# Dilated attention units issued one column tile earlier, with other PSUM banks and statistics in token order

## The chip, the cores and the metric

The kernel runs on one core of a Trainium2 chip. The metric is the device time of one execution in microseconds (us). Before the change it is 2284.05 us, the median of three runs (2281.86 to 2284.53).

## The reference, cut to what matters

A first block (a gated three-branch mixer over 512 tokens of width 1024) is followed by a second block of two layers. Only the attention part of each layer of the second block is touched:

```python
for l in range(2):
    h = rms_norm(x, norm_mix[l]); proj = h @ w_in[l]
    dq, dk, dv, sq, sk, sv, gate_logits = split(proj)      # dq, dk, dv: 3 groups x 4 heads x 64
    dq, dk = partial_rope(dq), partial_rope(dk)
    y_a = dilated_attention(dq, dk, dv) @ w_proj_a[l]       # merges 3 groups by softmax denominators
    y_b = stick_breaking_attention(sq, sk, sv) @ w_proj_b[l]
    gates = sigmoid(gate_logits + b_gate[l])
    mixed = gates[..., :1024] * y_a + gates[..., 1024:] * y_b
    x = x + mixed @ w_out[l]
    h = rms_norm(x, norm_ffn[l]); x = x + conv_ffn(h, ...)
```

Group 0 of the dilated attention looks at the last 129 tokens, group 1 at every 4th of the last 513, group 2 at every 16th. The kernel treats group 0 in token order, and groups 1 and 2 in "class" order: the tokens t = 4u + r with the same remainder r lie together.

## The kernel before, in words

Every big matrix product runs as three TensorE (PE) passes in fp32r, lines 1597 to 1599: weight-high by input-high, weight-high by input-low, weight-low by input-high. Weights come by DMA from the SyncE queue in chunks of two pieces (`chunk_load`); ScalarE (ACT) rounds a piece to its high half (`split_hi`, line 453), VectorE (DVE) subtracts to get its low half (`split_lo`, line 460), three pieces ahead of the tile that uses it. A piece is 24 matmuls of 512 columns (`col_tile`) or 48 of 256 columns (`token_tile`, for value tiles). Each engine's order of work is written out by hand; semaphores tie them. On PE, `give(bank, semaphore, value)` notes who reads a PSUM bank last, and the next `take(bank)` waits for that reader.

The order in a layer, on PE:

- 18 tiles (`DIL_KEYS`): six `dq`, six `dk`, six `dv` (two for each group 0, 1, 2). `dq` and `dk` tiles use banks 0 and 1 in turn; the value tiles of group 0 and of group 1 both use banks 0 and 1, those of group 2 use 4 and 5. Between them the stick-breaking attention of four heads runs: `sb_scores` (line 1807, banks 2 to 5), `sb_exponents` (1818, 1820), `sb_values` (1830, bank 6). ACT copies the value tiles out (line 882); those of groups 1 and 2 go to DRAM and come back in class order by a DMA from the POOL queue (line 621, awaited in `dil_values(0)`).
- `dil_scores(0)`, then eight units u (two head pairs j by four blocks b), two gate tiles each: gate tile 2u, `dil_transposes(u)` (line 1871), `dil_scores(u+1)` (1856, 1860), gate tile 2u+1, `dil_values(u)` (1889). Beside them DVE takes row maxima (`dil_max`, 1475 to 1478), ACT exponentiates (`dil_exp`, 905) and copies the transposed probabilities (`dil_pT`, 914). `dil_values` adds into bank 6 for group 0 (c = 0, 1) and bank 7 for groups 1 and 2 (c = 2, 3), both in blocks of 128 adjacent columns, so that bank 7 is in class order.
- In unit 7, `stat_rows` (1905) turns maxima and denominators into rows by 16 small matmuls. DVE's `shift_rows` and `share_rows` (1487 to 1503) and one ACT exponential make the two shares of each token, reordering between class and token order by strided reads and writes.
- Then the projections: `w_proj_b` half 0 (24 matmuls), `share_wide` (1917: four matmuls with 4 rows spread the shares over the partitions, banks 2 to 5), `w_proj_b` half 1, `w_proj_a` halves 0 and 1 (48 matmuls, line 1597 with `oaT`), and `row_tiles` of `w_out`. Between `share_wide` and `w_proj_a` lies a chain: ACT copies the wide shares from PSUM (941), DVE does a `split_lo`, then `dil_merge` (1509 to 1511) twice, ACT the high half (945), DVE the low half (`dil_lo`, 1515). Behind it DVE gates the `w_proj_b` results (1541), then those of `w_proj_a` (1547), adds both (1549), and takes the low half of the mix (1526).
- `w_proj_a` writes banks 2, 3, 4, 5, 0, 1, 6, 7 for m = 0 to 7. `row_tiles` first takes banks 0 to 3, so it waits until DVE has read m = 5 (line 1547).

## Time and profile before

| | us |
|---|---|
| runs, median (lowest to highest) | 2284.05 (2281.86 to 2284.53) |
| the profiled execution | 2284.14 |
| its span, first to last instruction | 2282.3 |
| PE busy | 2205.3 (97%) |
| DVE busy | 1258.1 (55%) |
| ACT busy | 779.2 (34%) |
| mean granted TensorE clock | 0.984 |

A busy PE is not PE at its peak: the ends of matmuls are modelled and overlap, so the pace of matmuls is read from the distance of their starts. The granted clock of 1.00 is 2.4 GHz, 0.50 is 1.2 GHz.

### The profile page before, as it was taken

The numbers are of one execution on the slowest core, as the hardware profiler recorded it, in microseconds if no ns is written. First come the engines' busy times: TensorE is split into PE (matmuls) and PEld (weight loads), VectorE is DVE, ScalarE is ACT, GpSimd is POOL, SyncE is SP. The second block draws the span as 40 slices with busy tenths as digits, with TensorE's granted clock in tenths as the row PEclk, the third lists the DMA queues.
The fourth block names the chain that finished last, engine by engine and source line by source line (L and its number), as shares of the span: only waits on it lengthen the run. The fifth ranks groups of instructions, "written<-read, shape, count | busy, mean of one in ns | idle before, by whom it ended". The sixth has DMA issues, their size and how long they took to land.

```text
span 2282.3 us, 25769 instructions
## 1 busy us (share of the span) xinstructions
PE 2205.3 (97%) x10730; PEld 1818.5 (80%) x10742; DVE 1258.1 (55%) x1662; ACT 779.2 (34%) x1112; POOL 35.4 (2%) x46
## 2 busy tenths in 40 slices
PE   3999999999999799999999999999999999999998
PEld 2788888888888697877788888889787768888887
DVE  7798797944655746323655554234632365555422
ACT  1223232223442344344343333134434424333211
POOL 1000000000000200000000000000000000000000
PEclk7999999999999899999999999999999989999999
DMA  8332322332222222222223223222222222332222
GB/s 303 116 103 90 108 97 79 111 110 94 88 97 97 74 93 74 90 79 73 74 75 111 92 94 107 86 83 93 74 94 78 69 74 74 101 103 93 95 99 74
DMA packets 188241, 217.91 MB, mean 95 GB/s; under 512 B 3808, under 2 KB 167262, under 8 KB 188126
## 3 DMA queue, kind: packets, MB, share of 16 engines
q1 hardware_dynamic: 184128, 210.52, 27.8%
q10 hardware_dynamic: 3262, 3.60, 0.5%
q8 instruction: 85, 1.39, 0.3%
q0 software_dynamic: 736, 2.15, 0.2%
q14 instruction: 30, 0.25, 0.0%
HBM read 212.06 MB, written 4.19 MB: 95 GB/s over the span
## 4 chain that ended last, share of the span: by engine, by line
PE 91%; DVE 6%; ACT 1%; issue 1%; POOL 0%; DMA 0%; SPq 0%; ACTq 0%; POOLq 0%; DVEq 0%
PE psum L1597 29%; PE psum L1599 28%; PE psum L1598 28%; DVE whl L460 1%; PE psum L1818 1%; DVE adsum L1038 1%; PE psum L1807 1%; PE psum L1830 1%; PE psum L1889 1%; PE psum L1860 1%; PE psum L1871 1%; DMA x<-in_x 0%; PE psum L1917 0%; DVE stat L1007 0%; ACT whl L453 0%
## 5 line engine op out<-in xcount | busy, mean ns | idle before, releaser
L1597 PE MATMUL psum<-hT,whl 128*128 128x512 f32 (+1 forms) x2112 | 804.4, 381 | 8.2 <-DVE hT L1060 5.4
L1598 PE MATMUL psum<-hT,whl 128*128 128x512 f32 (+1 forms) x2112 | 797.0, 377 | 0.0
L1599 PE MATMUL psum<-hT,whl 128*128 128x512 f32 (+1 forms) x2112 | 796.8, 377 | 0.0
L460 DVE TENSOR_TENSOR whl<-raw,whl 128x1024 fp32r<-128x1024 f32 (+1 forms) x368 | 449.3, 1223 | 594.4 <-ACT whl L453 594.4
L453 ACT ACTIVATE whl<-raw 128x1024 fp32r<-128x1024 f32 (+1 forms) x368 | 384.4, 1047 | 468.4 <-PE psum L1599 431.9
L1597 PEld LDWEIGHTS psum<-hT,whl 128*128 128x128 f32 x2112 | 399.0, 189 | 90.3 <-DVE hT L1060 8.9
L1599 PEld LDWEIGHTS psum<-hT,whl 128*128 128x128 f32 x2112 | 399.1, 189 | 73.4
L1598 PEld LDWEIGHTS psum<-hT,whl 128*128 128x128 f32 x2112 | 399.3, 189 | 71.3 <-issue 0.5
L1597 PE MATMUL psum<-whl,ff 128*128 128x512 f32 x352 | 139.2, 395 | 2.2 <-DVE fsil L1576 2.2
L1598 PE MATMUL psum<-whl,ff 128*128 128x512 f32 x352 | 138.9, 395 | 0.0
L1599 PE MATMUL psum<-whl,ff 128*128 128x512 f32 x352 | 138.9, 395 | 0.0
L1597 PE MATMUL psum<-whl,hT 128*128 128x256 f32 (+1 forms) x384 | 124.7, 325 | 10.3 <-DVE gates L1547 6.5
L1598 PE MATMUL psum<-whl,hT 128*128 128x256 f32 (+1 forms) x384 | 123.1, 321 | 0.0
L1599 PE MATMUL psum<-whl,hT 128*128 128x256 f32 (+1 forms) x384 | 123.0, 320 | 0.0
L1101 DVE SCALAR_TENSOR_TENSOR hc<-glu,vcol,hc 128x512 f32<-128x512 f32 x120 | 89.3, 744 | 0.0
L1597 PEld LDWEIGHTS psum<-whl,hT 128*128 128x128 f32 x384 | 73.6, 192 | 17.9 <-DVE gates L1547 7.3
L1567 DVE TENSOR_SCALAR facc<-apad,vcol 128x512 f32<-128x512 f32 x44 | 24.1, 547 | 110.9 <-ACT fsil L970 53.0
L1101 DVE SCALAR_TENSOR_TENSOR acc<-glu,vcol,acc 128x512 f32<-128x512 f32 x112 | 83.3, 744 | 0.1
L1597 PEld LDWEIGHTS psum<-whl,ff 128*128 128x128 f32 x352 | 66.3, 188 | 18.2 <-issue 3.0
L1598 PEld LDWEIGHTS psum<-whl,ff 128*128 128x128 f32 x352 | 66.3, 188 | 15.4
L1599 PEld LDWEIGHTS psum<-whl,ff 128*128 128x128 f32 x352 | 66.3, 188 | 15.4
L1599 PEld LDWEIGHTS psum<-whl,hT 128*128 128x128 f32 x384 | 73.7, 192 | 5.3
(270 smaller groups left out, 2159.4 us busy)
## 6 DMA issues: line engine op xcount, KB each, us to landing
raw<-in_w_in SPq DMA_DIRECT2D x88, 1024.0 KB, 5.1
raw<-in_w_up SPq DMA_DIRECT2D x44, 1024.0 KB, 5.1
raw<-in_w_down SPq DMA_DIRECT2D x20, 1024.0 KB, 5.1
ada<-in_w_ada SPq DMA_DIRECT2D x12, 1024.0 KB, 10.0
raw<-in_w_branch SPq DMA_DIRECT2D x12, 1024.0 KB, 5.1
raw<-in_w_out SPq DMA_DIRECT2D x12, 1024.0 KB, 5.0
x<-in_x SPq DMA_DIRECT2D x4, 512.0 KB, 6.7
v_by_token<-vnat ACTq DMA_DIRECT2D x4, 512.0 KB, 2.8
```

The source lines that it names most:

```text
L453: nc.scalar.activation(whl_view(w, 0), raw_view(w), ACT.Copy).then_inc(w_hi, 1)
L460: nc.vector.tensor_tensor(whl_view(w, 1), raw_view(w), whl_view(w, 0).bitcast(F), ALU.subtract).then_inc(w_lo, 1)
L1038: ins = V.scalar_tensor_tensor(o_, at_k(k), cact[:, k:k + 1], o_, ALU.mult, ALU.add)
L1101: last[dst is acc1] = step(V.scalar_tensor_tensor(A_(dst), g[:, k:k + SEQ], col("cf_w", 8 * k + tt), A_(dst), ALU.mult, ALU.add))
L1567: link(V.tensor_scalar(facc[:], apad[:, j, 2:2 + SEQ], cw(2), col("conv_b", FT * l + f), ALU.mult, ALU.add))
L1597: M(out_, stat_hi, mov_hi, start=start, stop=False, **kw)
L1598: M(out_, stat_hi, mov_lo, start=False, stop=False, **kw)
L1599: return M(out_, stat_lo, mov_hi, start=False, stop=stop, **kw)
L1807: M(bank(2 + kb)[:, 0:SEQ - kb * P], sbk[rows, h // 2, kb * P:(kb + 1) * P], sbq[rows, h // 2, kb * P:], start=True, stop=True, skip_group ...
L1818: M(bank(2 + kb)[:, (jb - kb) * P:SEQ - kb * P], (negtri_r if jb == kb else negones_r)[:], part[:, SBO[jb]:SBO[jb + 1]], start=False, stop ...
L1830: ins = M(bank(6)[po:po + HEAD, kb * P:], sbv[:, kb, h * HEAD:(h + 1) * HEAD], sba[:, SBO[kb]:SBO[kb + 1]], start=kb == 0, stop=kb == TB - ...
L1860: ins = M(bank(2 + e)[:, a:z], qd[heads, g, j, b * P:(b + 1) * P], kd[heads, g, j, k0:k0 + z - a], start=False, stop=g == 2, skip_group_ch ...
```

## The change

1. Value tiles come in the order of groups 1, 2, 0, and in banks 0 and 1, 6 and 7, 4 and 5. `dq` and `dk` tiles use banks 0 and 7. The stick-breaking output of head 3 goes to bank 0.
2. The dilated units are issued one column tile earlier: `dil_scores(0)` after value tile 16, `dil_transposes(0)` (into banks 6 and 7) and `dil_scores(1)` after value tile 17; then in unit u: gate tile 2u, `dil_values(u)`, gate tile 2u+1, `dil_transposes(u+1)`, `dil_scores(u+2)`. ACT's `dil_pT` and `dil_exp` and DVE's `dil_max` move with them.
3. `stat_rows` is cut in two: the maxima behind `dil_transposes(7)`, the denominators behind `dil_values(7)`, one gate tile before the projections. `share_rows` stands before the last `split_lo` of the gate tiles.
4. `dil_values` writes bank 7 in token order (a step of four elements in PSUM), and `stat_rows` does so for its second kind. The strided reads and writes on DVE go.
5. `dil_merge` reads the wide shares from PSUM: one product of 1024 elements and one sum per j in place of two products and a strided sum; ACT's copy (941) goes. Both merges stand before DVE's `split_lo`.
6. `w_proj_a` writes banks 2, 3, 0, 1, 4, 5, 6, 7.
7. In SBUF the constants and small tiles lie behind the scratch area in place of before it.

```diff
                 add("w_in_2", ("w_in_2", l, sec + g), [(name, l, g, j) for j in range(2)], 1024)
-        for g in range(3):
+        for g in (1, 2, 0):
...
-    PA_BANK = (2, 3, 4, 5, 0, 1, 6, 7)
+    PA_BANK = (2, 3, 0, 1, 4, 5, 6, 7)
+    SB_BANK = (6, 6, 6, 0)
+    PT_BANK = lambda u: 4 if u else 6
...
     def DIL_KEYS(l):
-        return [(name, l, g, j) for name in ("dq", "dk", "dv") for g in range(3) for j in range(2)]
+        return [(name, l, g, j) for name in ("dq", "dk", "dv") for g in ((1, 2, 0) if name == "dv" else (0, 1, 2)) for j in range(2)]
...
-        elif key[0] in ("dq", "dk", "gate"):
+        elif key[0] in ("dq", "dk"):
+            W_BANK[key] = 7 * key[-1]
+        elif key[0] == "gate":
...
         elif key[0] == "dv":
-            W_BANK[key] = 4 if key[2] == 2 else 0
+            W_BANK[key] = (4, 0, 6)[key[2]]
...
     whl = keep("whl", [P, 4, 2, 1024], R)
+    K = 1024
+    arena = at[0]
+    at[0] += ARENA
...
-    arena = (at[0] + 127) // 128 * 128
...
-    wide = over("wide", 12 * K, [P, 2, 2, SEQ])
+    wide = over("wide", 12 * K, [P, 2, SEQ])
...
+                    if n_ == 16:
+                        dil_exp(0)
+                    if n_ == 17:
+                        dil_pT(0)
+                        dil_exp(1)
 
                 for u in range(8):
                     split_hi(W[("gate", l, 2 * u)] + 3)
-                    dil_exp(u)
-                    if u == 4:
-                        dil_copy(0)
                     gate(2 * u)
-                    dil_pT(u)
+                    if u % 4 == 3:
+                        dil_copy(u // 4)
                     split_hi(W[("gate", l, 2 * u + 1)] + 3)
-                    if u == 7:
+                    gate(2 * u + 1)
+                    if u < 7:
+                        dil_pT(u + 1)
+                    if u < 6:
+                        dil_exp(u + 2)
+                    if u == 6:
                         act.wait_ge(row_x, l + 1)
                         A(mrow[0:4, 2:4, :], mrow[0:4, 2:4, :], ACT.Exp).then_inc(row_e, 1)
-                    gate(2 * u + 1)
-                dil_copy(1)
                 lead([("w_proj_b_2", l, 0)])
-                for j in range(2):
-                    act.wait_ge(wide_ps, 2 * l + j + 1)
-                    A(wide[:, j, :, :].rearrange("p a b -> p (a b)"), psum[:, (2 + 2 * j) * SEQ:(4 + 2 * j) * SEQ], ACT.Copy).then_inc(wide_in, 1)
                 lead([("w_proj_b_2", l, 1)])
                 for j in range(2):
                     act.wait_ge(oa_f, 2 * l + j + 1)
-                    A(oaT[:, j, 0, :], wide[:, j, 0, :], ACT.Copy).then_inc(oa_hi, 1)
+                    A(oaT[:, j, 0, :], wide[:, j, :], ACT.Copy).then_inc(oa_hi, 1)
...
-                    V.tensor_tensor(obT[po:po + HEAD, h // 2, 1, :], bank(6)[po:po + HEAD, :],
+                    V.tensor_tensor(obT[po:po + HEAD, h // 2, 1, :], bank(SB_BANK[h])[po:po + HEAD, :],
...
+                row = lambda i_: mrow[0:4, i_, :]
+
+                def shift_rows():
+
+                    dve.wait_ge(row_ps, 2 * l + 1)
+                    link(V.tensor_copy(row(0), bank(2)[0:4, :]))
+                    link(V.tensor_tensor(row(1), row(0), bank(3)[0:4, :], ALU.min))
+                    step(V.tensor_tensor(row(2), row(1), row(0), ALU.subtract))
+                    V.tensor_tensor(row(3), row(1), bank(3)[0:4, :], ALU.subtract).then_inc(row_x, 1)
+
+                def share_rows():
+
+                    dve.wait_ge(row_ps, 2 * l + 2)
+                    dve.wait_ge(row_e, l + 1)
+                    V.tensor_tensor(mrow[0:4, 0:2, :], mrow[0:4, 2:4, :], psum[0:4, 4 * SEQ:6 * SEQ].rearrange("p (a b) -> p a b", a=2),
+                                    ALU.mult).then_inc(den_used, 1)
+                    dve.wait_ge(den_used, l + 1)
+                    link(V.tensor_tensor(row(0), row(0), row(1), ALU.add))
+                    link(V.reciprocal(row(0), row(0)))
+                    step(V.tensor_tensor(row(4), row(2), row(0), ALU.mult))
+                    V.tensor_tensor(row(5), row(3), row(0), ALU.mult).then_inc(share, 1)
+
+                def dil_merge(j):
+
+                    dve.wait_ge(wide_ps, 2 * l + j + 1)
+                    dve.wait_ge(o_copied, 2 * l + j + 1)
+                    V.tensor_tensor(osb[j][:], osb[j][:], psum[:, (2 + 2 * j) * SEQ:(4 + 2 * j) * SEQ].rearrange("p (a b) -> p a b", a=2),
+                                    ALU.mult).then_inc(wide_used, 1)
+                    dve.wait_ge(wide_used, 2 * l + j + 1)
+                    V.tensor_tensor(wide[:, j, :], osb[j][:, 0, :], osb[j][:, 1, :], ALU.add).then_inc(oa_f, 1)
+
+                def dil_lo(j):
+                    dve.wait_ge(oa_hi, 2 * l + j + 1)
+                    V.tensor_tensor(oaT[:, j, 1, :], wide[:, j, :], oaT[:, j, 0, :].bitcast(F), ALU.subtract).then_inc(oa_lo, 1)
...
-
-                    dve.wait_ge(row_ps, 2 * l + 1)
-                    link(V.tensor_copy(by_token(row(0)), by_class(bank(3)[0:4, :])))
-                    link(V.tensor_tensor(row(1), bank(2)[0:4, :], row(0), ALU.min))
-                    step(V.tensor_tensor(row(2), row(1), bank(2)[0:4, :], ALU.subtract))
-                    V.tensor_tensor(row(3), row(1), row(0), ALU.subtract).then_inc(row_x, 1)
-
...
-                def share_rows():
-
-                    dve.wait_ge(row_ps, 2 * l + 2)
-                    dve.wait_ge(row_e, l + 1)
-                    step(V.tensor_tensor(row(1), row(2), bank(4)[0:4, :], ALU.mult))
-                    V.tensor_tensor(by_token(row(0)), by_token(row(3)), by_class(bank(5)[0:4, :]), ALU.mult).then_inc(den_used, 1)
-                    dve.wait_ge(dve_chain, chain[0])
-                    dve.wait_ge(den_used, l + 1)
-                    link(V.tensor_tensor(row(1), row(1), row(0), ALU.add))
-                    link(V.reciprocal(row(1), row(1)))
-                    step(V.tensor_tensor(row(4), row(2), row(1), ALU.mult))
-                    V.tensor_tensor(by_class(row(5)), by_token(row(3)), by_token(row(1)), ALU.mult).then_inc(share, 1)
-
-                def dil_merge(j):
-
-                    dve.wait_ge(wide_in, 2 * l + j + 1)
-                    dve.wait_ge(o_copied, 2 * l + j + 1)
-                    step(V.tensor_tensor(osb[j][:, 0, :], osb[j][:, 0, :], wide[:, j, 0, :], ALU.mult))
-                    link(V.tensor_tensor(osb[j][:, 1, :], osb[j][:, 1, :], wide[:, j, 1, :], ALU.mult))
-                    V.tensor_tensor(by_token(wide[:, j, 0, :]), by_token(osb[j][:, 0, :]), by_class(osb[j][:, 1, :]), ALU.add).then_inc(oa_f, 1)
...
+                    if n_ >= 16:
+                        dil_max(n_ - 16)
 
                 for u in range(8):
                     split_lo(W[("gate", l, 2 * u)] + 3)
-                    dil_max(u)
                     if u == 7:
+                        share_rows()
+                    split_lo(W[("gate", l, 2 * u + 1)] + 3)
+                    if u < 6:
+                        dil_max(u + 2)
+                    if u == 6:
                         shift_rows()
-                    split_lo(W[("gate", l, 2 * u + 1)] + 3)
-                share_rows()
+
                 def mixed_lo(m):
                     dve.wait_ge(mix_hi, 8 * l + m + 1)
                     V.tensor_tensor(hT[:, 1, m, :], gates[:, m, :], hT[:, 0, m, :].bitcast(F), ALU.subtract).then_inc(mix_lo, 1)
 
 
                 for j in range(2):
-                    split_lo(W[("w_proj_b_2", l, j)] + 3)
                     if j:
                         for jj in range(2):
                             dil_merge(jj)
+                    split_lo(W[("w_proj_b_2", l, j)] + 3)
+                    if j:
                         for jj in range(2):
                             dil_lo(jj)
...
                     pe.wait_ge(p_ready, 8 * l + u + 1)
-                    take(4, 5)
+                    tb = PT_BANK(u)
+                    take(tb, tb + 1)
...
-                            ins = nc.tensor.transpose(bank(4 + e)[:, c * P:(c + 1) * P], prob[:, e, c * P:(c + 1) * P], ident)
...
-                            ins = M(bank(6 + c // 2)[e * HEAD:(e + 1) * HEAD, b * P:(b + 1) * P], v, probT[:, e, c * P:(c + 1) * P],
+                            o_ = bank(6 + c // 2)[e * HEAD:(e + 1) * HEAD, :]
+                            o_ = o_[:, b * P:(b + 1) * P] if c < 2 else by_token(o_)[:, b, :]
+                            ins = M(o_, v, probT[:, e, c * P:(c + 1) * P],
                                     start=c in (first_, 2), stop=c in (1, 3), skip_group_check=True)
...
-                def stat_rows():
-
-                    pe.wait_ge(p_ready, 8 * l + 8)
-                    take(2, 3)
-                    for n_, columns in enumerate((nmax, den)):
-                        if n_:
-                            take(4, 5)
-                        for kind in range(2):
-                            for b in range(TB):
-                                ins = M(bank(2 + 2 * n_ + kind)[0:4, b * P:(b + 1) * P], columns[:, kind, b, :], ident, start=True, stop=True,
-                                        skip_group_check=True)
-                        ins.then_inc(row_ps, 1)
-                    give(2, row_x, l + 1)
-                    give(4, den_used, l + 1)
+                by_token = lambda ap: ap.rearrange("p (u r) -> p r u", r=TB)
+
+                def stat_rows(n_, columns):
+
+                    if n_ == 0:
+                        pe.wait_ge(p_ready, 8 * l + 8)
+                    take(2 + 2 * n_, 3 + 2 * n_)
+                    for b in range(TB):
+                        M(bank(2 + 2 * n_)[0:4, b * P:(b + 1) * P], columns[:, 0, b, :], ident, start=True, stop=True, skip_group_check=True)
+                    for r in range(TB):
+                        ins = M(by_token(bank(3 + 2 * n_)[0:4, :])[:, r, :], columns[:, 1, r, :], ident, start=True, stop=True, skip_group_check=True)
+                    ins.then_inc(row_ps, 1)
+                    give(2 + 2 * n_, *((den_used, l + 1) if n_ else (row_x, l + 1)))
...
@@ -1917,18 +1921,38 @@
                             ins = M(bank(2 + 2 * j + kind), sel[0:4, j, :], mrow[0:4, 4 + kind, :], start=True, stop=True)
                         ins.then_inc(wide_ps, 1)
                         for kind in range(2):
-                            give(2 + 2 * j + kind, wide_in, 2 * l + j + 1)
-
-                dil_scores(0)
+                            give(2 + 2 * j + kind, wide_used, 2 * l + j + 1)
+
+                for n_, key in enumerate(DIL_KEYS(l)):
+                    if key[0] == "dv":
+                        token_tile(key)
+                    else:
+                        col_tile(key, h_at(0), h_at(1))
+                    h, ph = n_ // 4, n_ % 4
+                    if ph == 0 and h >= 1:
+                        sb_values(h - 1)
+                    if ph == 0 and h < 4:
+                        sb_scores(h)
+                    if ph == 2 and h < 4:
+                        sb_exponents(h)
+                    if n_ == 16:
+                        dil_scores(0)
+                    if n_ == 17:
+                        dil_transposes(0)
+                        dil_scores(1)
+
                 for u in range(8):
                     col_tile(("gate", l, 2 * u), h_at(0), h_at(1))
-                    dil_transposes(u)
+                    dil_values(u)
+                    if u == 7:
+                        stat_rows(1, den)
+                    col_tile(("gate", l, 2 * u + 1), h_at(0), h_at(1))
                     if u < 7:
-                        dil_scores(u + 1)
-                    else:
-                        stat_rows()
-                    col_tile(("gate", l, 2 * u + 1), h_at(0), h_at(1))
-                    dil_values(u)
+                        dil_transposes(u + 1)
+                    if u < 6:
+                        dil_scores(u + 2)
+                    if u == 6:
+                        stat_rows(0, nmax)
```

## Rows read from the trace of the kernel before

**Rows 1.** Page, part 1 and part 4: busy time by engine, chain that ended last.
```profile
PE 2205.3 (97%) x10730; PEld 1818.5 (80%) x10742; DVE 1258.1 (55%) x1662; ACT 779.2 (34%) x1112; POOL 35.4 (2%) x46
PE 91%; DVE 6%; ACT 1%; issue 1%; POOL 0%; DMA 0%; SPq 0%; ACTq 0%; POOLq 0%; DVEq 0%
```
**Rows 2.** Waits of PE, whole span: waiting line, releaser: us in total, times, longest.
```profile
PE psum L1597 <- DVE gates L1547: 6.5, 2, 4.1
...
PE psum L1597 <- DVE oaT L1515: 3.1, 2, 2.2
PE psum L1597 <- ACT vd L882: 2.3, 2, 1.2
...
PE psum L1597 <- ACT qraw L873: 1.5, 2, 0.7
```
**Rows 3.** Timeline of PE, projections of layer 0: start, us, instructions [idle before, releaser].
```profile
1089.95 3.83 PE L1917 MATMUL psum<-mrow,cst 4*128 4x512 f32 x8
1093.71 0.80 PE L1597 MATMUL psum<-obT,whl 128*128 128x512 f32 x1
...
1103.09 0.51 PE L1597 MATMUL psum<-oaT,whl 128*128 128x512 f32 x1 [2.15 <-DVE oaT L1515]
...
1118.56 0.47 PE L1597 MATMUL psum<-whl,hT 128*128 128x512 f32 x1 [2.48 <-DVE gates L1547]
1118.86 0.39 PE L1598 MATMUL psum<-whl,hT 128*128 128x512 f32 x1
1119.09 0.40 PE L1599 MATMUL psum<-whl,hT 128*128 128x512 f32 x1
```
**Rows 4.** Timeline of PE, the same places of layer 1.
```profile
1831.01 4.20 PE L1917 MATMUL psum<-mrow,cst 4*128 4x512 f32 x8
1835.14 0.79 PE L1597 MATMUL psum<-obT,whl 128*128 128x512 f32 x1
...
1844.55 0.50 PE L1597 MATMUL psum<-oaT,whl 128*128 128x512 f32 x1 [0.94 <-DVE oaT L1515]
...
1860.02 0.76 PE L1597 MATMUL psum<-whl,hT 128*128 128x512 f32 x1 [4.06 <-DVE gates L1547]
```
**Rows 5.** Windows: stretch, us, busy PE PEld DVE ACT POOL, granted clock, DMA, GB/s.
```profile
1093.80:1103.00 9.20, 7.14 (x24) 5.40 (x24) 7.02 (x10) 3.92 (x5) 0.00 (x0) 0.84 0.00 0
1103.00:1118.50 15.50, 12.99 (x48) 10.10 (x48) 14.25 (x23) 4.38 (x7) 0.00 (x0) 0.89 0.20 68
...
1835.10:1844.50 9.40, 8.51 (x25) 6.37 (x24) 7.09 (x10) 3.96 (x5) 0.00 (x0) 0.69 0.00 1
...
1860.00:1875.00 15.00, 14.98 (x56) 12.18 (x57) 8.54 (x12) 4.96 (x6) 0.00 (x0) 0.84 0.20 71
```
**Rows 6.** Groups by form, 963 to 1132 us: busy us, mean ns, idle before, releaser.
```profile
L460 DVE TENSOR_TENSOR whl<-raw,whl 128x1024 fp32r<-128x1024 f32 x23 | 28.0, 1223 | 91.1 <-ACT whl L453 91.1
...
L1526 DVE TENSOR_TENSOR hT<-gates,hT 128x512 fp32r<-128x512 f32 x8 | 5.5, 685 | 0.1
...
L1511 DVE TENSOR_TENSOR wide<-osb 128x512 f32<-128x512 f32 x2 | 2.1, 1067 | 0.1
...
L1487 DVE COPY mrow<-psum 4x512 f32<-4x512 f32 x1 | 0.7, 678 | 5.1 <-PE psum L1905 5.1
```
**Rows 7.** Chain that ended last, in order of time: start, us, what.
```profile
993.26 1.02 PE psum L1889 x16
...
1073.94 3.59 PE psum L1905 x32
```
**Rows 8.** Timeline of DVE and ACT, layer 0, from the last value tiles to unit 0.
```profile
935.90 1.49 DVE L1451 TENSOR_TENSOR splo<-sbs,sphi 128x1280 fp32r<-128x1280 f32 x1 [1.70 <-ACT sphi L853]
...
967.54 0.42 DVE L1475 TENSOR_REDUCE stat<-psum 128x2 f32<-128x256 f32 x1
...
970.30 0.21 ACT L905 ACTIVATION_READ_ACCUMULATOR prob<-psum,stat 128x1 f32 x1
```
**Rows 9.** Page, part 6: DMA issues: count, KB each, us from issue to landing.
```profile
vc<-v_by_token POOLq DMA_DIRECT2D x4, 512.0 KB, 6.1
```

105 lines of the change are left out of this document (45 added, 60 removed).

## The prediction

> **What bounds the kernel now.** Read busy time and the chain first: PE is busy 97% of the span and makes 91% of the chain that ended last [rows 1]. So only what PE waits for, what PE itself does and its clock can move the time. The waits of PE come next: in the stages touched there are four, each once per layer [rows 2]. The timelines place them [rows 3, 4]: behind `share_wide`, w_proj_a waits for DVE's last low half of `oaT` (2.15 us in layer 0, 0.94 in layer 1), and `row_tiles` of w_out for the DVE line 1547 (2.48 and 4.06). The other two are the bank waits in front of value tiles: for ACT's copy of the tile before (line 882) and for `qraw` (line 873). Last the windows with the granted clock [rows 5]: behind `share_wide` and behind two of the waits PE runs partly at 0.50, the level of 1.2 GHz. The matmuls of 512 columns start 0.23 us apart at full clock (1118.86 to 1119.09 in rows 3).
>
> The sum is made against the profiled execution, 2284.14 us (span 2282.3 and 1.8 around it). The median of the runs is 2284.05, so the two need no correction.
>
> **Banks of the value tiles.** Group 1 starts in banks 0 and 1, whose last reader is now two tiles back (dk half 0; half 1 went to bank 7), so the 1.5 us for line 873 go. Group 2 goes to 6 and 7, group 0 to 4 and 5, last read by head 3's exponentials a tile earlier: the 2.3 us for line 882 go. Together **3.8 us** [rows 2]. What is late next: ACT now has to drain and issue the DMA of group 1 (two instructions) in front of head 3's `sphi`. DVE's `splo` comes behind it and ends at 937.4 [rows 8], while PE still has a value tile of 48 half-width matmuls, about 24 x 0.23 = 5.5 us, to run. A delay of well under 1 us there is hidden; if it were not, it would be paid once per layer. POOL's DMA back takes 6.1 us [rows 9] and starts two tiles earlier against its reader, so its cover grows.
>
> **Units one tile ahead.** No instruction is added or dropped on PE. In a unit the chain is scores, maxima, exponentials, transposes. From the first maximum to the end of the last exponential it took 970.5 - 967.5 = 3.0 us for unit 0 [rows 8], and about 4 us for a full unit. Before it had one gate tile (24 x 0.23 = 5.5 us) with a `split_lo` in front on DVE; now it has two tiles and `dil_values`, over 12 us. For unit 0 only value tile 17 is between, and DVE's `sb_out(3)` (0.7 us) stands in front: 0.7 + 3.0 is under 5.5. These chains cost PE next to nothing before, so I count 0 to 0.4 us, taken as **0**. The moved waits have work behind them: `dil_exp(u+1)` on ACT is in front of `split_hi` of a piece that PE wants three tiles later, over 16 us; the SyncE queue reloads `raw` behind that split, up to some 6 us later than before, and a chunk has that slack twice. `share_rows` on DVE (about 7 us, a 3.3 us reciprocal in it) stands in front of the split of the first w_proj_a piece, wanted after w_proj_b and `share_wide`, over 12 us later. The shares are ready a gate tile earlier; `share_wide` did not wait before, so this alone gives nothing.
>
> **The merge chain.** Let P be the start of `share_wide` (1089.95). Before, w_proj_a started at P + 13.1. Now DVE starts at P + 2.0 with a product of 1024 elements from PSUM. Its price is bounded by `split_lo` of that size, 1.22 us [rows 6], and twice that; I take the first, since a DVE copy of 512 elements from PSUM takes 0.68 like a sum of 512 from SBUF [rows 6]. Product 1.2 and sum 0.7 (without the stride: 0.69 for 1.07, rows 6), twice: P + 5.9. `split_lo` 1.2, two low halves 0.6 each: P + 8.4. PE ends `share_wide` at P + 3.76 [rows 3] and needs 24 x 0.23 = 5.5 more for w_proj_b: P + 9.3, at half clock later. So DVE is done 0.9 us before PE asks: the 3.1 us go.
>
> **Banks of w_proj_a.** `row_tiles` takes banks 0 to 3, read now by m = 0 to 3 and not m = 5. DVE: four gatings of w_proj_b until P + 11, a split to P + 12.2, then three instructions of about 0.63 us per m. It has read m = 3 by P + 18, and the second low half of the mix, which the first block wants, is there by P + 17.3. PE arrives at P + 9.3 + 11.1 = P + 20.4. The later low halves come every 1.9 us; PE uses two in 5.5 us. So the 6.5 us go too. Sum of both waits: **9.6 us** [rows 2].
>
> **The clock behind the waits.** Lost time in a window is (1 - granted) x length. Layer 0, w_proj_a behind its wait: 0.11 x 15.5 = 1.7 us; layer 1, w_out behind the 4.06 us: 0.16 x 15.0 = 2.4 us [rows 5]. The clock fell after PE had stood still, so without the waits I take back all: **4.1 us**; the bounds are 0 and 4.1. Behind `share_wide` the loss is 0.16 x 9.2 = 1.5 and 0.31 x 9.4 = 2.9 us [rows 5]. Its 4-row matmuls stay, so I leave these 4.4 us; they could go (-4.4), or double (+4.4).
>
> **Token order written by PE.** Half of the value instructions and half of the statistics now write PSUM with a step of four elements. No row shows such a write. Priced at a factor f: a unit's 16 value instructions take 1.02 us and the 32 of the statistics 3.59 [rows 7], so (0.51 x 8 + 1.80) x 2 layers = 11.8 us x (f - 1). Below 1 is excluded: the instructions and columns are the same. From above, DVE's strided write to SBUF is 1067 ns for 685, f = 1.56 [rows 6]: 6.6 us; and the strided read from PSUM cost nothing (678, line 1487). I take f = 1: the statistics' instruction takes 3.59 / 32 = 112 ns for 128 columns, twice the time per column of the 512-column ones (0.23 us), so a write at half pace would still keep up. That is the weakest step.
>
> The Trainium skill speaks against it (Advanced Engine Details and Errata, section PSUM Cachelines): PSUM lines hold two fp32 values, and a non-contiguous pattern "significantly slows down matmuls". It gives no factor. No row here shows it right or wrong.
>
> **Constants behind scratch.** Addresses alone; the tiles of one operation in different buffers take the same time in all rows read. 0.
>
> **Sum.** 3.8 + 9.6 + 4.1 = 17.5; 2284.14 - 17.5 = 2266.6, and **2266.5 us** against the median.
>
> **Rivals.**
> - Strided writes cost moderately, f from 1.5 to 2. For: DVE's row; the token-order write is read out of no row. Against: the slow pace per column of these instructions. 2266.5 + 5.9 to 11.8 = 2272 to 2278.
> - Slower than before: strided writes cost much. It decides from 11.8 x (f - 1) = 17.5, f = 2.5. At f = 4 (every fourth element, four times the lines) it is +35.4: 2302 us. Against: nothing in the rows comes near it. This is where the skill's rule would lead if "significantly" is a factor over 2.5.
> - The wait only moves: w_proj_a or w_out still waits for DVE, because the merge chain has 0.9 us to spare and a late share or a PSUM product at double price (+2.4 us) eats it. Half of 9.6 stays, and with it the 4.1 of clock: 2266.5 + 8.9 = 2275.
> - The clock goes otherwise behind `share_wide`: 4.4 us back, 2262; or 4.4 more, 2271.
>
> **How the numbers follow.** Forecast 0.52; moderate cost 0.18; wait moves 0.12; clock otherwise 0.11 (0.07 down, 0.04 up); slower 0.07. The forecast's own range is 2263 to 2270. Eight in ten: 2262 to 2278, which leaves out the slow rival and the ends of the others. A measurement of this kernel can't tell under 0.2%, 4.6 us, from no change. Faster, under 2279.5: all but the slow rival and a mix of costs, 0.88. Same 0.05, slower 0.07.
>
> **What would show it.** Waits of PE on lines 873, 882, 1515 and 1547 gone in both layers; w_proj_a starting about 9.5 to 12 us after `share_wide` starts, and w_out 11.1 us later; clock 1.00 in both windows. In the chain of waits, 16 instructions of `dil_values` still at 1.02 us and the statistics at 1.8 us a half: any more is f. Wrong would be: a new PE wait on `prob` or `probT` between gate tiles, on `whl` (a split or a chunk late), or on `vc`.

## The result, and the profile after

The changed kernel takes 2254.14 us (median of 4 runs, 2253.38 to 2254.63) against 2283.06 (2281.86 to 2284.53) of the kernel before beside it: a ratio of 0.9873, 95% interval 0.9856 to 0.989. It is faster, and by more than forecast: 2254.1 lies below the range of 2262 to 2278. The profiled execution took 2254.25 (span 2252.4), 29.9 us less than the one of before.

Page of the kernel after, parts 1 and 4 (they answer to [rows 1]):

```profile
PE 2188.2 (97%) x10742; PEld 1816.0 (81%) x10742; DVE 1257.7 (56%) x1656; ACT 775.2 (34%) x1108; POOL 35.4 (2%) x46
PE 92%; DVE 5%; issue 1%; ACT 1%; DMA 1%; POOL 0%; SPq 0%; POOLq 0%; DVEq 0%; ACTq 0%
```

PE's busy time fell by 17.1 us. Waits that go don't lower busy time; matmuls that no longer run at half clock do, and so does a faster pace. The runs told of below part the two: the change without its layout has 2199.1 us of PE busy, the layout alone 2195.3.

Waits of PE, whole span, after (answers to [rows 2]; columns as there). The lines shown were there before and lie outside the change; the four of [rows 2] are gone:

```profile
PE psum L1725 <- DVE adsum L1048: 13.7, 4, 4.8
...
PE psum L1611 <- DVE hT L1070: 6.1, 4, 4.4
PE psum L1611 <- DVE fsil L1590: 2.2, 2, 1.1
PE psum L1611 <- POOL hT L612: 1.5, 1, 1.5
PE psum L1611 <- DVE whl L467: 0.9, 3, 0.3
PE psum L1729 <- DVE stat L1061: 0.5, 1, 0.5
```

Timeline of PE and DVE in the projections of layer 0, after (answers to [rows 3]; the three passes are now lines 1611 to 1613):

```profile
1082.48 4.88 PE L1921 MATMUL psum<-mrow,cst 4*128 4x512 f32 x8
1087.29 0.80 PE L1611 MATMUL psum<-obT,whl 128*128 128x512 f32 x1
1087.88 0.63 PE L1612 MATMUL psum<-obT,whl 128*128 128x512 f32 x1
...
1094.94 0.39 PE L1611 MATMUL psum<-oaT,whl 128*128 128x512 f32 x1
...
1105.82 0.39 PE L1611 MATMUL psum<-whl,hT 128*128 128x512 f32 x1
```
```profile
1084.49 1.22 DVE L1504 TENSOR_TENSOR osb<-osb,psum 128x1024 f32<-128x1024 f32 x1 [1.22 <-PE psum L1921]
...
1087.39 1.22 DVE L1504 TENSOR_TENSOR osb<-osb,psum 128x1024 f32<-128x1024 f32 x1 [0.95 <-PE psum L1921]
...
1090.39 1.29 DVE L1511 TENSOR_TENSOR oaT<-wide,oaT 128x512 fp32r<-128x512 f32 x2
```

The product from PSUM takes the 1.22 us that was chosen for it. The last low half of `oaT` ends at 1091.7, 3.3 us before PE starts w_proj_a at 1094.94, and w_out follows 10.88 us later with no wait (11.1 was forecast). Counted from the start of `share_wide`, DVE is ready after 9.2 us (8.4 forecast) and PE asks after 12.5 (9.5 to 12 forecast): `share_wide` took 1.1 us longer than before, and the passes behind it ran at half clock.

Windows of the projections, after (columns as in [rows 5], which they answer to). Behind `share_wide` the clock is still at half; in w_proj_a and w_out it is now 1.00 in both layers:

```profile
1087.00:1092.00 5.00, 5.00 (x13) 3.71 (x13) 4.57 (x6) 0.73 (x2) 0.00 (x0) 0.53 0.00 0
...
1817.00:1822.00 5.00, 5.00 (x13) 3.92 (x12) 4.43 (x7) 0.63 (x1) 0.00 (x0) 0.50 0.00 0
```
```profile
1094.90:1105.80 10.90, 10.90 (x49) 9.02 (x49) 9.02 (x14) 4.54 (x6) 0.00 (x0) 1.00 0.28 96
1105.80:1120.80 15.00, 15.00 (x68) 12.41 (x67) 12.94 (x17) 5.50 (x7) 0.00 (x0) 1.00 0.19 57
1824.60:1835.50 10.90, 10.90 (x49) 9.03 (x49) 8.99 (x14) 4.54 (x6) 0.00 (x0) 1.00 0.26 96
1835.50:1850.50 15.00, 15.00 (x68) 12.39 (x67) 12.96 (x17) 5.50 (x7) 0.00 (x0) 1.00 0.17 60
```

The writes in token order can be read in one kernel, side by side. Timeline of PE, the statistics of the maxima, after (answers to [rows 7]): line 1909 writes adjacent columns, line 1911 every fourth.

```profile
1061.01 1.04 PE L1909 MATMUL psum<-cst,stat 128*4 128x128 f32 x8
1061.88 1.04 PE L1911 MATMUL psum<-cst,stat 128*4 128x128 f32 x8
```

Both take 1.04 us, and the 16 value instructions stand in the chain of waits at their old 1.02:

```profile
980.53 1.02 PE psum L1894 x16
```

What is left is in stages that no edit touches. Tile `ff` (the input of the second half of the feed-forward), the kernel before and then the kernel after: durations in ns, lowest, median and highest, of the passes that read it:

```profile
L1597 PE MATMUL psum<-whl,ff x352: 390/393/475, 1408.6 to 2274.4; 128*128 128x512 f32 x176
```
```profile
L1611 PE MATMUL psum<-whl,ff x352: 387/389/476, 1395.7 to 2244.5; 128*128 128x512 f32 x176
```

The durations are modelled, so the number to read is how many start in equal time. Window of these matmuls alone, before and then after: stretch, us, PE busy (count), clock, DMA, GB/s:

```profile
1420.00:1470.00 50.00, 50.00 (x217) 1.00 0.28 95
```
```profile
1420.00:1470.00 50.00, 50.00 (x223) 1.00 0.29 95
```

That is 6 more passes in the same 50 us at the same granted clock: their starts are 232 ns apart before and 227 after (medians over 1055 distances, each from a pass on `ff` to the matmul behind it). The 1055 distances add to 245.5 us before and 239.6 after, 2.4% less.

Where the 30 us went, by the starts of matmuls on PE (us, layers 0 and 1 together; worked out from the profiled executions, one of each kernel. "Start" is the first pass with a weight tile, 53 us into the span. The other columns are the runs told of below):

```
stretch                                        before   after  layout  no layout  banks   banks   merge
                                                               only    (e2)       w_proj  value   only
                                                               (e1)               (e7)    (e8)    (e9)
start to the stick-breaking of layer 0         781.8   776.9   776.9   781.7     781.9   781.9   782.1
stick-breaking scores to share_wide            510.5   504.4   510.3   504.8     510.5   505.3   510.4
share_wide to w_out                             57.6    46.6    58.0    45.7      51.2    59.2    50.9
w_out to the first pass on ff                  582.4   579.8   584.1   579.9     580.0   583.1   585.5
first pass on ff to the next layer / the end   297.2   291.4   291.4   297.2     297.2   298.2   297.2
sum                                           2229.5  2199.1  2220.7  2209.3    2220.7  2227.7  2226.1
```

### The profile page after: what moved, and what is told of

It reads as the page before. It is cut to its first block, busy times and chain, and to the rows that moved or that the text cites. A ratio compares the mean times of both kernels' runs of the same rounds, so it can differ in the third digit from the quotient of the medians.

```text
span 2252.4 us, 25769 instructions
## 1 busy us (share of the span) xinstructions
PE 2188.2 (97%) x10742; PEld 1816.0 (81%) x10742; DVE 1257.7 (56%) x1656; ACT 775.2 (34%) x1108; POOL 35.4 (2%) x46
## 4 chain that ended last, share of the span: by engine, by line
PE 92%; DVE 5%; issue 1%; ACT 1%; DMA 1%; POOL 0%; SPq 0%; POOLq 0%; DVEq 0%; ACTq 0%
PE psum L1611 29%; PE psum L1612 29%; PE psum L1613 29%; PE psum L1832 1%; DVE adsum L1048 1%; PE psum L1821 1%; PE psum L1845 1%; DVE whl L467 1%; PE psum L1862 1%; PE psum L1894 1%; PE psum L1874 1%; PE psum L1921 0%; DMA x<-in_x 0%; DVE stat L1017 0%; POOL stat L617 0%
## 5 line engine op out<-in xcount | busy, mean ns | idle before, releaser
L1611 PE MATMUL psum<-whl,ff 128*128 128x512 f32 x352 | 137.3, 390 | 2.2 <-DVE fsil L1590 2.2
L1612 PE MATMUL psum<-whl,ff 128*128 128x512 f32 x352 | 137.0, 389 | 0.0
L1613 PE MATMUL psum<-whl,ff 128*128 128x512 f32 x352 | 137.0, 389 | 0.0
L1611 PEld LDWEIGHTS psum<-whl,ff 128*128 128x128 f32 x352 | 66.1, 188 | 16.7 <-issue 3.0
L1611 PEld LDWEIGHTS psum<-whl,hT 128*128 128x128 f32 x384 | 73.2, 191 | 5.4
L1613 PEld LDWEIGHTS psum<-whl,ff 128*128 128x128 f32 x352 | 66.1, 188 | 13.8
L1613 PEld LDWEIGHTS psum<-whl,hT 128*128 128x128 f32 x384 | 73.1, 190 | 5.0
L1612 PEld LDWEIGHTS psum<-whl,hT 128*128 128x128 f32 x384 | 73.2, 191 | 5.0
```

The source lines that it names most:

```text
L1611: M(out_, stat_hi, mov_hi, start=start, stop=False, **kw)
L1612: M(out_, stat_hi, mov_lo, start=False, stop=False, **kw)
L1613: return M(out_, stat_lo, mov_hi, start=False, stop=stop, **kw)
```

## The experiments

The kernel before ran beside each group of runs and gave medians of 2285.91 (the runs up to the one with all 128 up), 2282.19 (64 up and the parts alone) and 2286.18 (256 up, the probe and the split). Its single executions lie between 2281.6 and 2287.9, so a difference of a few us between two kernels is read from the ratio and its interval, not from two medians.

**The layout alone.** Theory: point 7 of the change made the passes faster. Rival: something else in the change did.

```diff
+    ARENA = 80 * 1024 + 16704 + 2112
...
     whl = keep("whl", [P, 4, 2, 1024], R)
+    arena = at[0]
+    at[0] += ARENA
...
-    arena = (at[0] + 127) // 128 * 128
```

> The kernel before with point 7 of the change alone: the scratch area directly behind the weight buffers, constants and small tiles behind it. Theory A (the miss of the prediction is this point): in the trace before, 512-column passes whose one operand lies in the scratch area start 232 to 233 ns apart, those with both operands outside it 227 ns; after, all are at 227. This kernel then gains about 12 us: 2283 to about 2271, and its passes on yahl and ff start 227 ns apart, while the four PE waits of the prediction stay. Theory B (the layout is nothing, and the extra came from units one tile ahead or from the merge): no change, 2283.

Measured: 2276.01 us, ratio 0.996 (0.9946 to 0.9974). The window of `ff`:

```profile
1420.00:1470.00 50.00, 50.00 (x223) 1.00 0.28 95
```

The pace is the one of after, and two of the table's stretches (the first, and the one from `ff` on) fall by the same 4.9 and 5.8 us as in the change. Its waits stay. The stretch from `w_out` to `ff` is 1.7 us longer; that is the clock, and the kernels with other addresses, told of below, show that such a difference comes and goes with no change in the order of work.

**The change without the layout.**

```diff
-    arena = at[0]
-    at[0] += ARENA
...
+    arena = (at[0] + 127) // 128 * 128
```

> The kernel after with point 7 undone: constants in front, scratch area where it was. Theory A: the rest of the change is worth what the prediction summed, 17.5 us, so about 2266, and the passes on yahl and ff are back at 232 ns. Theory B: stays at 2254.

Measured: 2263.27 us, ratio 0.9904 (0.9889 to 0.9918). `ff` is back at the old pace:

```profile
1420.00:1470.00 50.00, 50.00 (x216) 1.00 0.27 95
```

By the sums of the table, points 1 to 6 give 20.2 us and point 7 gives 10.2; the forecast had 17.5 and 0. By the medians and ratios of the runs, points 1 to 6 give 22 (18.7 to 25.4), and the layout 9 to 12 (2263.27 against 2254.14; and the layout alone and the two kernels with 128 bytes, told of next, against the kernel before).

**What about the addresses?** By the kernel's allocation, `hT` begins at byte 32896 of a partition and `whl` at 82048, both 128 above a multiple of 256. The scratch area (`ff`, the mixer's tiles, `oaT`, `obT`) begins at 128000 before, a multiple of 256, and at 114816 after, 128 above one. Theory A1 (A1a in some of the expectations): what counts is the distance of a matmul's two operands modulo 256 bytes (128 is slow, 0 is fast). A1b: what counts is the absolute place of the one in scratch. Four kernels before, with the scratch area moved by 128 and 256 and 64 bytes, and with everything moved by 128 and scratch on a multiple of 256.

```diff
-    arena = (at[0] + 127) // 128 * 128
+    arena = (at[0] + 127) // 128 * 128 + 128
```

> The kernel before with the scratch area 128 bytes higher and nothing else. Before, the scratch area starts at a multiple of 256 bytes and hT and the weight buffers 128 bytes behind one. Theory A1 (the pace hangs on the addresses modulo 256): all passes at 227 ns, about 2271. Theory A2 (it hangs on where the scratch area lies in the memory as a whole, above or beside the constants): no change, 2283.

```diff
-    base = (nc.sbuf_base + 63) // 64 * 64
+    base = (nc.sbuf_base + 63) // 64 * 64 + 128
...
-    arena = (at[0] + 127) // 128 * 128
+    arena = (at[0] + 255) // 256 * 256
```

> The kernel before with x, hT, raw and the weight buffers 128 bytes higher, so that they start at multiples of 256 bytes, and the scratch area at a multiple of 256 too. Theory A1a (both operands of a pass must have the same address modulo 256, whichever it is): all passes at 227 ns, about 2271. Theory A1b (the absolute address counts: an operand at a multiple of 256 is slow): now every pass on hT is slow as well, 5568 + 384 of 512 columns at 5 ns each, some 30 us more than before, about 2313.

```diff
-    arena = (at[0] + 127) // 128 * 128
+    arena = (at[0] + 127) // 128 * 128 + 256
```

> The kernel before with the scratch area 256 bytes higher alone: distance from hT and the weight buffers 128 bytes modulo 256 as before, but every address of it moved twice as far as in the 128-byte run. Theory A1 (period of 256 bytes): passes on ff and yahl stay at 232 ns, time about 2283. Rival (any move off the old place helps, the old place being bad for another reason): 227 ns, about 2272.

```diff
-    arena = (at[0] + 127) // 128 * 128
+    arena = (at[0] + 127) // 128 * 128 + 64
```

> The kernel before with the scratch area 64 bytes higher alone; its distance from hT and the weight buffers is then 192 bytes modulo 256. Theory A1a in its plain form (only a distance of 0 modulo 256 is fast): passes with one operand in the scratch area stay at about 232 ns, time about 2283. Rival (any distance but 128 is fast, or distance 0 modulo 64 is all that counts): 227 ns and about 11 us less.

Measured, the window of `ff` in each. Scratch 128 up (2274.6 us, ratio 0.9954, 0.9938 to 0.997), then all 128 up (2273.79, 0.9951, 0.9935 to 0.9967):

```profile
1420.00:1470.00 50.00, 50.00 (x222) 1.00 0.30 98
```
```profile
1420.00:1470.00 50.00, 50.00 (x222) 1.00 0.28 96
```

Scratch 256 up (2282.35 us, one execution), then 64 up (2280.84, one execution):

```profile
1420.00:1470.00 50.00, 50.00 (x217) 1.00 0.28 95
```
```profile
1420.00:1470.00 50.00, 50.00 (x220) 1.00 0.29 95
```

128 bytes alone bring the whole gain (10.7 us from the first matmul to the last), and 256 bytes bring none. With everything 128 up, scratch is again on a multiple of 256, where it was slow before, and the pace is fast: A1b falls, A1 stands. The 64 bytes gave `ff` a pace between the two (229 ns median; the 1055 distances add to 241.8 us), which neither form of the theory had in it, while the tiles of the mixer stayed at 233: it is not a matter of two cases.

One tile of the scratch area tests A1 once more, inside single kernels. `poolhl` lies 64 bytes above a multiple of 256 where the rest of scratch lies on one. Its 512-column passes start 233.4 ns apart in the kernel before (64 bytes below `whl` modulo 256) and 230.8 in the kernel after (64 above), so it never was at the best pace. With scratch 64 up it comes to distance 0 as the only scratch tile, and there it is at 226.7 ns, beside 233.3 for `yahl` in the same kernel (means of 40 and 176 distances).

These kernels also show how far the clock moves by itself. The order of work between `share_wide` and `ff` is that of the kernel before in the layout alone and in the four address kernels, and the two stretches together took 640.0 us (before), 642.1 (layout alone), 639.4 (128 up), 642.0 (all 128 up), 637.1 (256 up) and 639.9 (64 up): 5.0 us from the lowest to the highest, of which the address effect makes about 1. Windows of PE in layer 1, the kernel before and then 256 up (stretch, us, PE busy (count), clock, DMA, GB/s):

```profile
1820.00:1880.00 60.00, 55.00 (x217) 0.89 0.20 70
```
```profile
1820.00:1880.00 60.00, 55.54 (x230) 0.94 0.21 71
```

The kernel after does the same in its two profiled executions: 626.4 us, and 624.8 when it was run again. So of a single execution's stretches between `share_wide` and `ff`, a difference of 2 us or so is not the edit's until more runs show it.

**The parts that take waits away, each alone.** First the banks of w_proj_a (point 6):

```diff
-    PA_BANK = (2, 3, 4, 5, 0, 1, 6, 7)
+    PA_BANK = (2, 3, 0, 1, 4, 5, 6, 7)
```

> The kernel before with point 6 alone (w_proj_a writes banks 2, 3, 0, 1, 4, 5, 6, 7). By the prediction: the waits of 2.48 and 4.06 us in front of w_out go and the half clock behind the second, 2.4 us, with them: 8.9 us less. Rival: w_out then waits for the low halves of the mix in place of the banks (the wait only moves), and at most 2 to 4 us are gained.

Measured: 2275.9 us (2274.35 to 2278.04), ratio 0.997 (0.9957 to 0.9982), which is 4 to 10 us. The sum of the table falls by 8.8 us, as expected. The wait for the gatings is gone, and `w_out` to `ff` is 2.4 us shorter with no half clock behind `w_out`; but with scratch 256 up, where that wait stayed (4.9 us in two), there was none behind `w_out` either, so these 2.4 us are not shown to be the edit's. The wait for `oaT` stays, and the clock is at half for a while behind it in layer 0 (0.89), not in layer 1 (1.00). Waits of PE, then the windows behind that wait in either layer:

```profile
PE psum L1597 <- DVE oaT L1515: 3.5, 2, 2.1
```
```profile
1103.00:1118.00 15.00, 14.53 (x56) 11.70 (x57) 13.78 (x21) 4.45 (x7) 0.00 (x0) 0.89 0.20 70
...
1845.00:1860.00 15.00, 15.00 (x67) 12.21 (x66) 13.75 (x21) 4.75 (x7) 0.00 (x0) 1.00 0.20 71
```

Then the banks of the value tiles (point 1):

```diff
+    SB_BANK = (6, 6, 6, 0)
...
-        elif key[0] in ("dq", "dk", "gate"):
+        elif key[0] in ("dq", "dk"):
+            W_BANK[key] = 7 * key[-1]
+        elif key[0] == "gate":
...
-            W_BANK[key] = 4 if key[2] == 2 else 0
+            W_BANK[key] = (4, 0, 6)[key[2]]
```

> The kernel before with point 1 alone (order and banks of the value tiles, banks of dq and dk, bank of head 3). By the prediction 3.8 us less; measured from start to start instead of by idle time, the two gaps are 1.44 - 0.12 and 1.12 - 0.23 us, so 2.2 us a layer, 4.4 us less. Rival: the two DMAs now issued by ACT earlier delay head 3 and eat it: 0 to 2 us.

Measured: 2281.39 us (2280.01 to 2283.29), ratio 0.9993 (0.9983 to 1.0002): by the runs no difference that can be told. Its own stretch falls by 5.2 us in the table, more than expected, but the profiled execution is 3.3 us longer elsewhere: the projections by 1.6, `w_out` to `ff` by 0.7, the last stretch by 1.0. In the projections it is the clock, which here falls inside `share_wide` already, as it did in the layout alone, where no bank was changed. That the value banks cause it is not shown, and the last stretch is not explained. Windows of layer 0, this kernel and then the one before:

```profile
1089.00:1094.00 5.00, 5.00 (x11) 2.23 (x10) 0.00 (x0) 2.47 (x3) 0.00 (x0) 0.68 0.30 115
1094.00:1099.00 5.00, 5.00 (x16) 3.98 (x15) 4.41 (x6) 1.15 (x2) 0.00 (x0) 0.64 0.00 0
```
```profile
1089.00:1094.00 5.00, 5.00 (x14) 2.19 (x13) 1.40 (x3) 1.21 (x2) 0.00 (x0) 0.94 0.60 209
1094.00:1099.00 5.00, 5.00 (x17) 3.95 (x17) 3.15 (x4) 1.78 (x2) 0.00 (x0) 0.72 0.00 0
```

Last the merge chain (point 5):

```diff
-                for j in range(2):
-                    act.wait_ge(wide_ps, 2 * l + j + 1)
-                    A(wide[:, j, :, :].rearrange("p a b -> p (a b)"), psum[:, (2 + 2 * j) * SEQ:(4 + 2 * j) * SEQ], ACT.Copy).then_inc(wide_in, 1)
...
-                    step(V.tensor_tensor(osb[j][:, 0, :], osb[j][:, 0, :], wide[:, j, 0, :], ALU.mult))
-                    link(V.tensor_tensor(osb[j][:, 1, :], osb[j][:, 1, :], wide[:, j, 1, :], ALU.mult))
+                    V.tensor_tensor(osb[j][:], osb[j][:], psum[:, (2 + 2 * j) * SEQ:(4 + 2 * j) * SEQ].rearrange("p (a b) -> p a b", a=2),
+                                    ALU.mult).then_inc(wide_in, 1)
```

> The kernel before with point 5 alone, in class order: dil_merge multiplies 1024 elements straight from PSUM, ACT's copy goes, both merges stand before split_lo; the strided sum stays. By the prediction's chain the low halves are ready 4.6 us earlier, w_proj_a no longer waits, and w_out still waits for the bank of m = 5, but that comes 4.6 us earlier too: 7 to 10 us less. Points 5 and 6 share one DVE chain, so their separate gains sum to more than both together (13.7 by the prediction). Rival: the product from PSUM costs double, 2.4 us later: 3 to 5 us less.

Measured: 2281.74 us (2278.71 to 2284.18), ratio 0.9989 (0.998 to 0.9998), far less than expected. The wait for `oaT` goes, and from `share_wide` to w_out 6.7 us go with it. But w_out is reached earlier against the same gatings and waits 3.24 us in layer 0, where it was 2.48 (in layer 1 3.2, where it was 4.06; 6.5 in all as before). Behind it the clock is at half in both layers, before in layer 1 alone. Timeline of PE at that place and the window behind it:

```profile
1116.32 0.77 PE L1596 MATMUL psum<-whl,hT 128*128 128x512 f32 x1 [3.24 <-DVE gates L1546]
1116.88 0.63 PE L1597 MATMUL psum<-whl,hT 128*128 128x512 f32 x1
```
```profile
1117.00:1122.00 5.00, 5.00 (x13) 3.85 (x12) 4.84 (x8) 2.41 (x4) 0.00 (x0) 0.50 0.00 0
```

13 matmuls are counted in these 5 us, where 23 or so would be at 227 ns. `w_out` to `ff` is 3.2 us longer than before. Over the two stretches from `share_wide` to `ff`, points 5 and 6 alone so give 3.6 and 8.8 us, 12.4 in all; with both in (e2) they give 14.4, 625.6 against 640.0. That difference of 2.0 us is within what the clock does by itself, so these sums don't show that the parts need one another.

The times of the runs say it better. The three parts alone have ratios of 0.9993, 0.9970 and 0.9989, some 11 us in all; points 1 to 6 together have 0.9904, some 22, and points 2 to 4 show no gain of that size in any stretch. So the parts are worth more together than one by one. The reading that fits is that the half clock comes back only when the last wait near it goes: PE was at half clock between `share_wide` and `ff` for 20.5 us in the kernel before, 13.7 in e7, 23.9 in e8, 20.5 in e9 and 10.2 in e2, and half of such a time is lost. It rests on one execution of each, and 256 up had 13.7 with both waits in place; so it is argued, not shown.

**A probe of step and offset.** In front of w_proj_b, additional matmuls whose results nobody reads: 64 in bf16 with 256 adjacent columns in PSUM, 64 with every second column; then nine blocks of 32 in fp32r with 448 columns, with the stationary and the moving operand begun at various columns of `hT` (4 bytes each).

```diff
+                for o_ in (bank(6)[:, 0:256], bank(6).rearrange("p (n t) -> p t n", t=2)[:, 0, :]):
+                    for _ in range(64):
+                        M(o_, identb[:], maskb[:, 0:256], start=True, stop=True, skip_group_check=True)
+                for so, mo in ((0, 0), (0, 8), (0, 16), (0, 24), (0, 32), (0, 48), (0, 64), (32, 0), (32, 32)):
+                    for _ in range(32):
+                        M(bank(6)[:, 0:448], hT[:, 0, 0, so:so + P], hT[:, 1, 2, mo:mo + 448], start=True, stop=True, skip_group_check=True)
```

> The kernel after with matmuls added in front of w_proj_b in each layer, their results not used. First 64 bf16 matmuls of 256 columns to adjacent PSUM columns and 64 to every second column. If a step of two costs (each element on its own 8-byte line), the second 64 start about twice as far apart, some 215 ns for 107; if not, both take the same. Then nine blocks of 32 fp32r matmuls of 448 columns, stationary and moving operand both in hT, with the moving one 0, 32, 64, 96, 128, 192 and 256 bytes further, then the stationary one 128 bytes further, then both. Theory A1: with distance 0 and 256 and with both moved the starts are 448/512 of 227 ns apart, 198 to 199; with 128 bytes, whichever operand moves, some 2% more, 203; 64 and 192 bytes between or above. Rival (the absolute address of one operand counts): the block with both moved is slow too, and one of the two 128-byte blocks is fast.

Measured (2409.81 us, one execution; what counts are the windows, one for each block, in order: bf16 adjacent, bf16 every second, then the nine offsets):

```profile
1077.95:1084.95 7.00, 7.00 (x65) 6.27 (x65) 3.43 (x4) 1.63 (x2) 0.00 (x0) 1.00 0.34 106
1084.95:1098.58 13.63, 13.63 (x66) 8.78 (x65) 0.00 (x0) 0.00 (x0) 0.00 (x0) 1.00 0.07 26
1098.58:1105.25 6.67, 6.67 (x34) 6.21 (x33) 0.00 (x0) 0.00 (x0) 0.00 (x0) 1.00 0.00 0
1105.25:1111.87 6.62, 6.62 (x33) 6.02 (x32) 0.00 (x0) 0.00 (x0) 0.00 (x0) 1.00 0.00 0
1111.87:1118.26 6.39, 6.39 (x33) 5.99 (x32) 0.00 (x0) 0.00 (x0) 0.00 (x0) 1.00 0.00 0
...
1124.83:1131.36 6.53, 6.53 (x33) 6.01 (x32) 0.00 (x0) 0.00 (x0) 0.00 (x0) 1.00 0.00 0
...
1137.82:1144.43 6.61, 6.61 (x33) 6.01 (x32) 0.00 (x0) 0.00 (x0) 0.00 (x0) 1.00 0.00 0
```

The step costs a factor of 1.97 here: starts are 109.3 ns apart with adjacent columns and 215.2 with a step of two, the same in both layers. So a stepped write does cost, where a matmul writes a column in 0.43 ns. With the step it takes 0.84 ns for each, and the fp32 statistics, at 109 ns for 128 columns, take 0.85 with or without one. This fits the reason that the prediction gave for f = 1: a write at half pace keeps up with these matmuls. The two sides differ in more than pace, though (bf16 and a step of two, fp32 and a step of four). By the Trainium skill (Advanced Engine Details and Errata, section PSUM Cachelines) a non-contiguous pattern slows matmuls significantly: the bf16 rows agree, the fp32 rows of this kernel don't. fp32r matmuls with a step were not tried.

The offsets matter in the probe too, with paces from 200.0 to 206.7 ns, but not as A1 has it (the windows shown are those of 0, 8, 16, 32 and 64 columns): no offset took 202.7, 16 columns (64 bytes) 200.0, 32 columns (128 bytes) 203.7, and 64 columns (256 bytes) 206.7, as slow as any. With both operands begun 32 columns further it was 206.5, where the same distance without the shift took 202.7. Here every matmul loads the same stationary tile, where the passes of the kernel change it. So A1 holds for the passes of this kernel, by five layouts and `poolhl`, and is no general law; why the addresses matter stays open.

**share_wide in two halves.** To break up the stretch of 4-row matmuls: two of the four behind half of w_proj_b half 0, two behind its end.

```diff
-                def share_wide():
+                def share_wide(j):
...
+                        if mm == 2 and between is not None:
+                            between()
...
-                projection("w_proj_b_2", 0, PB_BANK, obT, pb_ps, pb_f)
-                share_wide()
+                projection("w_proj_b_2", 0, PB_BANK, obT, pb_ps, pb_f, lambda: share_wide(0))
+                share_wide(1)
```

> The kernel after with share_wide cut in two: the four matmuls of j = 0 (with 4 rows each) between the second and third quarter of the first half of w_proj_b, those of j = 1 behind that half. After, PE runs at 0.50 of its clock behind share_wide in both layers and loses 2.4 and 3.4 us there. If the unbroken 4 us of nearly empty matmuls bring the clock down, the two halves of 2 us do not, and 4 to 6.5 us are gained: about 2248 to 2250 against the kernel after on the same chip. If their sum counts, nothing is gained.

Measured: 2251.96 us (2249.1 to 2256.1), ratio 0.9856 (0.9841 to 0.9871). Beside it, the kernel after once more:

> The kernel after unchanged, for comparison with the others on the same chip: 0.987 of the kernel before.

2254.08 us (2253.35 to 2254.71), ratio 0.9865 (0.9848 to 0.9881): the result repeats to 0.1 us. The two can't be told apart. The half clock does not go; it comes behind either half, and the windows of layer 0's projections show both:

```profile
1084.00:1089.00 5.00, 5.00 (x13) 2.80 (x12) 2.45 (x3) 1.06 (x1) 0.00 (x0) 0.75 0.36 139
1089.00:1094.00 5.00, 5.00 (x16) 3.91 (x16) 4.93 (x8) 1.26 (x2) 0.00 (x0) 0.66 0.00 0
```

In its profiled execution, the slowest of its four, the way from the first pass of w_proj_b to w_out is 29.25 us in layer 0 and 29.27 in layer 1; in the kernel after it is 28.87 and 28.79, and in that kernel run again 28.80 and 27.24. The others of the split ran at a mean clock of 0.988 to 0.99 against its 0.986, so the split may let the clock come back earlier at times; that is argued from the clocks, not shown.

## Why the prediction was wrong, point by point

**The step that failed** is the one on constants behind scratch: "Addresses alone; the tiles of one operation in different buffers take the same time in all rows read. 0." The runs showed 10.2 us in its place (e2 against the kernel after; 9 to 12 by the runs), since the passes on the scratch area run faster with both operands at the same place modulo 256 bytes. The trace of before did hold the difference: passes on `ff` and on the mixer's tiles start 232 ns apart and those on `hT` 227, with the same shape, clock and type. The prediction read 0.23 us off two rows on `hT` [rows 3], and to two decimals both paces are the same. 5 ns over the 2064 passes that read a scratch tile are 10 us. The sum over all 1055 distances on `ff`, divided by their count, would have shown it. Which way a new layout would turn this was not to be known from one trace, but that it could move by about 10 us either way was, and no rival had it.

**Banks of the value tiles**: 3.8 forecast, 5.2 measured in their own stretch (e8). The waits went as described. The size was off since an idle time in a row of waits is counted from the modelled end of the matmul before, not from the start that it could have had: for line 882 the row has 1.16 us, while the start comes 1.44 behind the last one where 0.12 is the pace, so 1.32. Likewise the 0.73 us for line 873 are 0.89 by starts. About 0.3 us per layer more lies between the first dilated scores and values and was not traced.

**Units one tile ahead**: 0 forecast. With these points, the stepped writes among them, the stretch is 0.5 us shorter than with the banks alone (504.8 in e2, 505.3 in e8), which one execution of each can't tell from nothing. Right.

**The merge chain, the banks of w_proj_a and the clock behind the waits**: 9.6 + 4.1 = 13.7 forecast, 14.4 measured from `share_wide` to `ff` (e2). The waits went as described. The agreement to 0.7 us is in part luck, since kernels with one order of work differ by up to 5 us over these stretches. The margin in front of w_proj_a was 3.3 us and not 0.9, because PE came late, and not because DVE was early: DVE was 0.8 us later than forecast, its second product having waited 0.95 us for `share_wide`. At full clock PE would have asked 9.3 us after the start of `share_wide` by the forecast's sum, and DVE was ready at 9.2. The half clock behind `share_wide` stayed, as forecast, at 0.53 and 0.50 in windows of 5 us.

**Token order written by PE**: f = 1, the "weakest step", is right, 1.04 us for 8 with or without the step. The rival of f = 2.5 and more is out, and the moderate one too. The bf16 blocks show that it was no safe bet: at twice this pace per column a step of two costs a factor of 1.97. The rival's f = 4 had no ground in the line of two values that the prediction quotes, though: with a step of four each value has a line to itself, which is twice as many lines as adjacent columns take, and not four times.

**The chances.** Points 1 to 6 alone gave 2263.27 us, at the lower end of the forecast's own range of 2263 to 2270; their ratio of 0.9904 would give 2262.1 from 2284.05. The range of 2262 to 2278 had no term for the step that failed, and with one of ±10 it would have held the result.

## What to carry to other kernels

Read paces as sums of many distances of starts, divided by their count, and compare them between tiles of one shape: a few ns between two tiles that do the same came from their addresses here, and were worth 0.4%. A change that moves the layout of SBUF can move every matmul, so its edit has a price with both signs until it is measured; with this kernel's passes it was best to keep both operands at the same place modulo 256 bytes. Where two waits of PE stand close behind one another, expect less from taking away one than its share of the sum, and run the unchanged kernel more than once before a difference of 2 us behind a wait is called the edit's.

## What the runs showed of the hardware

- fp32r passes of 512 columns start 232 to 233 ns apart when their operands lie 128 bytes apart modulo 256, and 227 at distance 0. At 64 below `whl` modulo 256 it is 229 for `ff` and 233 for the mixer's tiles, and at 64 above it 231 for `poolhl`. With one stationary tile loaded again and again, 448 columns took 200.0 to 206.7 ns by offset, in another order.
- bf16 matmuls of 256 columns: 109.3 ns with adjacent columns in PSUM, 215.2 with a step of two. fp32 matmuls of 128 columns: 109 ns with adjacent columns and with a step of four.
- 3.2 us in which PE stood still were followed by 5 us at a granted clock of 0.50 (e9), and so were 4.9 us of 4-row matmuls (after, 0.53). Two such stretches half as long did it too, with 0.75 and 0.66. The 2.48 us of layer 0 in the kernel before were not followed by any (1.00 from 1118 to 1133).
- Kernels with one order of work between `share_wide` and `ff` were at half clock there for 13.7 to 23.9 us, which is 5 us of time between the ends.
